# Modulation rows summed on VectorE from tiles turned through DRAM, in place of sum and bias products on TensorE

## The reference, cut to what matters

```python
def modulation(silu_cond, w_mod_l, b_mod_l):
    m = silu_cond @ w_mod_l + b_mod_l            # (1024) @ (1024, 6144) + (6144)
    return jnp.split(m[:, None, :], 6, axis=-1)

def run_layer(x, silu_cond, lw, rope, ctx):
    sh1, sc1, g1, sh2, sc2, g2 = modulation(silu_cond, lw['w_mod'], lw['b_mod'])
    out, ctx_tensors = token_mixer(modulate(x, lw['norm1'], sh1, sc1), lw, rope, ctx)
    x = x + g1 * out
    x = x + g2 * moe_ffn(modulate(x, lw['norm2'], sh2, sc2), lw)
    return x, ctx_tensors
```

## Time and profile before

| What | Value |
|---|---|
| median of three runs | 1472.4 us |
| profiled execution, its own time | 1473.27 us |
| its span | 1471.3 us |
| TensorE busy | 1327.3 us (90%) |
| VectorE, ScalarE, GpSimd busy | 476.2, 328.4, 256.9 us |
| weight loads on SyncE's queue | 327.33 MB, 58.6% of 16 engines' span |
| mean granted clock of TensorE | 0.986 |

### The profile page before, as it was taken

How to read it: one execution, slowest core, us unless ns; L and a number is a source line. 1 busy time by engine, 2 the same in 40 slices (tenths; PEclk the granted TensorE clock), 3 DMA queues, 4 the chain that set the end, 5 groups by cost and what they waited for, 6 DMA issues and landing times.

```text
span 1471.3 us, 17933 instructions
## 1 busy us (share of the span) xinstructions
PE 1327.3 (90%) x7009; PEld 746.0 (51%) x7010; DVE 476.2 (32%) x855; ACT 328.4 (22%) x505; POOL 256.9 (17%) x225
## 2 busy tenths in 40 slices
PE   6999999999999977689899999999999988997772
PEld 2655446675545443345446554555654554553341
DVE  2424326762144101111144352576413521110003
ACT  2136416631001000000021662464100110000001
POOL 2620017721001000000037000683100010000001
PEclk9999999999999999999999999999999999999996
DMA  9781426553829899999973221466412589999994
GB/s 346 257 295 66 172 86 218 212 186 143 281 102 380 336 396 396 396 395 390 361 252 125 94 82 57 173 230 228 158 58 114 224 348 379 405 389 391 399 412 178
DMA packets 105726, 371.90 MB, mean 253 GB/s; under 512 B 7376, under 2 KB 22064, under 8 KB 89280
## 3 DMA queue, kind: packets, MB, share of 16 engines
q1 hardware_dynamic: 84816, 327.33, 58.6%
q0 software_dynamic: 6928, 23.98, 4.5%
q10 hardware_dynamic: 13920, 19.74, 3.9%
HBM read 341.60 MB, written 29.43 MB: 252 GB/s over the span
## 4 chain that ended last, share of the span: by engine, by line
PE 75%; DMA 17%; DVE 4%; ACT 1%; issue 1%; SPq 1%; ACTq 0%; POOL 0%; DVEq 0%; POOLq 0%
PE pG L1587 25%; PE pG L1579 10%; DMA ring<-in_w_exp_down_dram 9%; PE pS L1676 8%; PE pG L1828 6%; PE pG L1692 5%; DMA hT_gen<-in_w_exp_up_dram 3%; DMA ring<-in_w_exp_up_dram 3%; PE pG L1540 3%; PE pX L1507 2%; PE pX L1676 2%; DMA ring<-in_w_mod_dram 2%; PE pX L1656 2%; PE pS L1656 2%; PE pS L1601 2%; PE pX L1642 1%
## 5 line engine op out<-in xcount | busy, mean ns | idle before, releaser
L1587 PE MATMUL pG<-hT_gen,ring 128*128 128x384 f32 x1024 | 339.6, 489 | 1.6 <-ACT hT_gen L955 1.6
L1587 PEld LDWEIGHTS pG<-hT_gen,ring 128*128 128x128 f32 x1024 | 191.8, 190 | 134.5 <-issue 6.6
L1676 PE MATMUL pS<-ring,hT_gen 128*64 128x256 f32 x1408 | 160.1, 383 | 27.6 <-DMA ring<-in_w_exp_up_dram 15.2
L1579 PE MATMUL pG<-ring,hT_gen 128*128 128x512 f32 (+1 forms) x384 | 148.7, 543 | 1.8 <-DVE hT_gen L1112 1.6
L1676 PEld LDWEIGHTS pS<-ring,hT_gen 128*64 128x64 f32 x1408 | 101.8, 138 | 91.9 <-DMA ring<-in_w_exp_up_dram 19.7
L1467 DVE TENSOR_TENSOR hT_gen<-pS,hT_gen 128x256 f32<-128x256 f32 x32 | 19.3, 602 | 371.2 <-PE pS L1676 371.2
L1579 PEld LDWEIGHTS pG<-ring,hT_gen 128*128 128x128 f32 x384 | 71.5, 190 | 70.0 <-issue 64.3
L741 POOL DMA_INDIRECT hT_gen<-y_scr,idx x12 | 11.4, 950 | 515.3 <-ACTq L1020 512.2
L1692 PE MATMUL pG<-ring,hT_gen 128*64 128x512 f32 x352 | 82.1, 608 | 18.6 <-issue 8.2
L982 ACT COPY hT_gen<-pG 128x512 f32<-128x512 f32 x32 | 18.8, 586 | 300.2 <-PE pG L1692 300.2
L1828 PE MATMUL pG<-ring 128*128 128x512 f32 x192 | 83.3, 593 | 2.5 <-DVE ring L1351 2.5
(11 more groups left out here) (282 smaller groups left out, 1643.9 us busy)
## 6 DMA issues: line engine op xcount, KB each, us to landing
ring<-in_w_mod_dram SPq DMA_DIRECT2D x24, 2048.0 KB, 8.2
ring<-in_w_exp_up_dram SPq DMA_DIRECT2D x22, 2048.0 KB, 33.6
ring<-in_w_exp_down_dram SPq DMA_DIRECT2D x22, 2048.0 KB, 34.9
ring<-in_w_exp_gate_dram SPq DMA_DIRECT2D x22, 2048.0 KB, 27.6
ring<-in_w_in_dram SPq DMA_DIRECT2D x20, 2048.0 KB, 7.9
modb<-in_w_exp_gate_dram SPq DMA_DIRECT2D x10, 2048.0 KB, 34.2
hT_gen<-in_w_exp_up_dram SPq DMA_DIRECT2D x10, 2048.0 KB
rows_nw<-in_w_exp_down_dram SPq DMA_DIRECT2D x10, 2048.0 KB, 38.2
```

The lines of the kernel that those rows point to most:

```text
L1579: ins = pe.matmul(ps[:, 0:width], hT[:, k, t * P:(t + 1) * P], w[:, k, 0:width], start=(k == 0), stop=(k == KC - 1))
L1587: ins = pe.matmul(ps[:, 0:TOK], w[:, k, c0:c0 + P], src[:, k, :], start=(k == 0), stop=(k == nk - 1))
L1676: ins = pe.matmul(dst[64 * hf:64 * hf + 64, 0:256], x[:, k, :], w[:, k, 256 * hf:256 * (hf + 1)], start=(k == 0), stop=(k == KC - 1))
```

## The change

The row tiles lose their sum product, and their bias products. The four partial sums of a row tile stay in `modb` as before; ScalarE stores eight rows of it (four parts, two conditions) to a scratch tensor in DRAM (`parts_store`), loads them back turned, so that 64 partitions hold 8 columns each of one condition and 64 those of the other (`parts_load`, two DMAs of 256 pieces of 32 bytes), VectorE adds the four parts and the bias (`mod_rows`), and ScalarE stores the two rows to `mod_scr` (`row_store`, two DMAs of 64 pieces). In the loop over levels the three stages of a tile stand 1, 2 and 5 steps behind its products, VectorE's sum 4. The bias of the row tiles is loaded at the start in four further DMAs of GpSimd. Column tiles are as before.

```diff
...
 def mod_groups(first, last):
-    return [(kind, m + i) for m in range(first, last, 2) for kind in ("mod", "ms") for i in range(2)]
+    return [("mod", m) for m in range(first, last)]
 def groups(L):
     def after(m):
-        return ("mc" if m in COL_MODS else "ms", m)
-    gs = [g for m in range(MOD_FIRST) for g in (("mod", m), after(m))] if L == 0 else []
+        return [("mc", m)] if m in COL_MODS else []
+    gs = [g for m in range(MOD_FIRST) for g in [("mod", m)] + after(m)] if L == 0 else []
...
-        gs += [("ga", j)] + [after(m - 1)] * (j > 0) + [("mod", m)]
-    return (gs + [after(m)] + [("wba", j) for j in range(KC)] + [(k, j) for j in range(KC) for k in ("gh", "wbh")]
+        gs += [("ga", j)] + (after(m - 1) if j > 0 else []) + [("mod", m)]
+    return (gs + after(m) + [("wba", j) for j in range(KC)] + [(k, j) for j in range(KC) for k in ("gh", "wbh")]
...
 O_BANK = (6, 7, 2)
-SMALL_LOADS = 16 * 9
+SMALL_LOADS = 16 * 13
...
+    part_scr = nc.dram_tensor("part_scr", [2, 4, 2, 512], F32, kind="Internal").ap()
+        mparts = sb("mparts", [P, 2, 4, 8])
+        mrow = sb("mrow", [P, 2, 8])
+        mbias = sb("mbias", [P, DEPTH, 8, 8])
...
                             pool.dma_start(dst[:, l, :], a[name][l:l + 1, :].broadcast_to([P, w])).then_inc(small_in, 16)
                     pool.dma_start(wr[:, :, :], a["w_router"].rearrange("(p k) e -> p k e", p=P)).then_inc(small_in, 16)
                     pool.dma_start(br[:, :], a["b_router"].rearrange("(a e) -> a e", a=1).broadcast_to([P, NE])).then_inc(small_in, 16)
+                    for l in range(DEPTH):
+                        for cnd in range(2):
+                            pool.dma_start(mbias[64 * cnd:64 * (cnd + 1), l, :, :],
+                                           a["b_mod"][l, 512 * MOD_FIRST:512 * MODS].rearrange("(u j i) -> j u i", j=64, i=8)
+                                           ).then_inc(small_in, 16)
                     pool.dma_start(masks[:, :, :].rearrange("p s t -> p (s t)"), a["masks"]).then_inc(small_in, 16)
                 pool.wait_ge(h_ready, 2 * NT * L + NT)
...
                 elif m >= 2:
-                    act.wait_ge(mod_stored[m % 2], mods_stored(m, m % 2))
+                    act.wait_ge(part_out[m % 2], 16 * rows_before(m, m % 2))
                 act.copy(mod_parts(m), ps).then_inc(mod_evac, 1)
-            def mod_store(L, m):
-                ps = sync_group(L, ("ms", m))
-                r = 32 * (m % 2)
-                act.copy(mod_parts(m)[r:r + 32, :], ps[r:r + 32, :]).then_inc(ms_evac, 1)
-                act.wait_ge(ms_evac, ROW_MODS.index(m) + 1)
+            def parts_store(m):
+                b = m % 2
+                act.wait_ge(mod_evac, m + 1)
+                act.wait_ge(part_in[b], 32 * rows_before(m, b))
+                act.dma_start(part_scr[b].rearrange("q c n -> (q c) n"),
+                              modb[0:P:16, 2, 0, 512 * b:512 * (b + 1)]).then_inc(part_out[b], 16)
+            def parts_load(m):
+                b = m % 2
+                act.wait_ge(part_out[b], 16 * (rows_before(m, b) + 1))
+                act.wait_ge(mod_summed, max(ROW_MODS.index(m) - 1, 0))
                 for cnd in range(2):
-                    dst = mod_scr[m // MODS, cnd:cnd + 1, 512 * (m % MODS):512 * (m % MODS + 1)]
-                    act.dma_start(dst, mod_parts(m)[r + 16 * cnd:r + 16 * cnd + 1, :]).then_inc(mod_stored[m % 2], 16)
+                    act.dma_start(mparts[64 * cnd:64 * (cnd + 1), b, :, :],
+                                  part_scr[b, :, cnd, :].rearrange("q (j i) -> j q i", i=8)).then_inc(part_in[b], 16)
+            def row_store(m):
+                b = m % 2
+                act.wait_ge(mod_summed, ROW_MODS.index(m) + 1)
+                for cnd in range(2):
+                    dst = mod_scr[m // MODS, cnd, 512 * (m % MODS):512 * (m % MODS + 1)]
+                    act.dma_start(dst.rearrange("(j i) -> j i", i=8),
+                                  mrow[64 * cnd:64 * (cnd + 1), b, :]).then_inc(mod_stored[b], 16)
+            def rows_step(L, i):
+                for delay, stage in ((1, parts_store), (2, parts_load), (5, row_store)):
+                    m = MOD_LEV * (L + 1) + i - delay
+                    if 0 <= i - delay < KC and m in ROW_MODS:
+                        stage(m)
+            def rows_behind(L, kind, stage):
+                if L == 0:
+                    for m in range(MOD_BEHIND[kind], MOD_BEHIND[kind] + 2):
+                        stage(m)
             def mods_behind(L, kind):
...
                     m = MOD_BEHIND[kind]
                     mod_copy(L, m)
                     mod_copy(L, m + 1)
-                    mod_store(L, m)
-                    mod_store(L, m + 1)
+                    parts_store(m)
+                    parts_store(m + 1)
             def hT_half(n, t):
                 act.wait_ge(hT_made, 2 * NT * n + 2 * t + 2)
...
                         att(L, ATT_AT[(kind, h)])
+                        if h == 1:
+                            rows_behind(L, "hq", (parts_load, row_store)[d])
                     mods_behind(L, kind)
                     act.wait_ge(f_done, 2 * HH * L + HH * (d + 1))
                     if d == 0:
...
                     ps = sync_group(L, ("i", t))
                     act.copy(v_rows[:, t, :], ps).then_inc(vrow_ready, 1)
...
+                    if t == 1:
+                        rows_behind(L, "fb", parts_load)
                 mods_behind(L, "i")
                 for t in range(NT):
...
                     act.activation(sg[:, t, :], ps, ACT.Sigmoid).then_inc(sig_done, 1)
                     if ("g", t) in ATT_AT:
...
+                rows_behind(L, "fb", row_store)
                 for j in range(KC):
                     ps = sync_group(L, ("ga", j))
                     act.activation(mergedT[:, j, :], ps[:, 0:TOK], ACT.Sigmoid).then_inc(ga_ready, 1)
                     m = MOD_LEV * (L + 1) + j
-                    if j > 0 and m - 1 in ROW_MODS:
-                        mod_store(L, m - 1)
+                    rows_step(L, j)
                     lev(L, j + 1)
                     mod_copy(L, m)
-                if m in ROW_MODS:
-                    mod_store(L, m)
+                rows_step(L, KC)
                 act.wait_ge(lv_mm, LEV_TILES * L + NT * (LEV_STEPS - 1))
                 act.activation(E[1].rearrange("p (s t) -> p s t", s=SEG), Cs[1][:, :, 0:128], ACT.Exp)
                 for d in range(2):
                     ins = act.activation(dec[:, d, :], Cs[d][:, :, 128], ACT.Exp)
                 ins.then_inc(fin_E, 1)
+                rows_step(L, KC + 1)
                 act.wait_ge(fin_D, 2 * L + 1)
                 act.activation(E[0], E[0], ACT.Exp).then_inc(fin_E, 1)
+                rows_step(L, KC + 2)
                 act.wait_ge(lv_mm, LEV_TILES * (L + 1))
                 act.activation(W[1].rearrange("p (s t) -> p s t", s=SEG), Cs[0][:, :, 1:129], ACT.Exp).then_inc(fin_E, 1)
                 act.wait_ge(fin_D, 2 * L + 2)
                 act.activation(W[0], W[0], ACT.Exp).then_inc(fin_E, 1)
+                rows_step(L, KC + 3)
+                rows_step(L, KC + 4)
                 act.wait_ge(st_ready, 4 * L + 2)
                 for d in range(2):
                     dst = (new_sf, new_sb)[d][0, L].rearrange("h k v -> k h v")
...
                     ins = dve.scalar_tensor_tensor(dst, ps, 1.0, bc(nwT[:, l, k0:k0 + 4], [P, 4, 2], 2),
                                                    ALU.add, ALU.mult)
                 ins.then_inc(mc_evac, 1)
+            def mod_rows(m):
+                b, l = m % 2, m // MODS
+                dve.wait_ge(part_in[b], 32 * (rows_before(m, b) + 1))
+                dve.wait_ge(mod_stored[b], mods_stored(m, b))
+                link(dve.tensor_reduce(mrow[:, b, :], mparts[:, b, :, :].rearrange("p q i -> p i q"), AX.X, ALU.add))
+                dve.tensor_tensor(mrow[:, b, :], mrow[:, b, :], mbias[:, l, m % MODS - MOD_FIRST, :],
+                                  ALU.add).then_inc(mod_summed, 1)
+            def mod_rows_of(L, j):
+                m = MOD_LEV * (L + 1) + j
+                if m in ROW_MODS:
+                    mod_rows(m)
             def norm1_mean(L, t):
                 dve.wait_ge(sq_done, NT * 2 * L + t + 1)
...
                         dve.tensor_scalar(x, x, omT[:, L, d, h:h + 1], lbT[:, L, d, h:h + 1], ALU.mult,
                                           ALU.add).then_inc(f_done, 1)
                         att(L, ATT_AT[(kind, h)])
+                    if L == 0 and d == 0:
+                        for m in range(MOD_BEHIND["hq"], MOD_BEHIND["hq"] + 2):
+                            mod_rows(m)
                     dve.wait_ge(ln_done, 2 * L + d + 1)
                     for s in range(SEG):
                         dve.tensor_tensor_scan(Cs[d][:, s, 1:129], ones, scratch[:, s * P:(s + 1) * P], 0.0,
...
```

(28 more changed lines are left out.)

9 lines of the change are left out of this document (6 added, 3 removed).

## The result

| | before | after |
|---|---|---|
| median of 7 runs each, in turns on one chip, us | 1473.14 (1471.92 to 1475.96) | 1479.09 (1476.53 to 1480.83) |
| ratio, 95% interval | | 1.0033 (1.002 to 1.0046) |
| profiled execution: span, us | 1471.3 | 1476.7 |
| VectorE instructions / packets on ScalarE's DMA queue | 855 / 13920 | 887 / 25376 |

A forecast was written before the change was run, and what follows sets the result against it. TensorE was taken to bound projections and loops, DMA the experts. Gains of 4.5, 3.8 and 4.1 us (12.4) less 3.6 lost made 8.8 us faster: 1463.5 us, range 1457.5 to 1471.5.

The forecast's parts named there:

- the pairs in layer 0: Row tiles 4 to 7, two pairs in layer 0's projections, where TensorE is full: 4.5 us gained without sums and bias products.
- the start: Four bias loads on GpSimd ahead of the masks; delay up to some 8 us hidden by gaps: 0.4 us lost.
- rival (b): Small bias pieces at the start are dear, each microsecond beyond 8 us of delay is lost; chance 0.08.
- the cost behind layer 0's loop: Two issues on ScalarE behind layer 0's loop over levels: 0.5 us lost.
- the upper end of my sum (16): Whole kernel: the favourable ends of all terms together give 16 us gained, the other ends 1 us.
- the clock: Longer TensorE idle behind both loops lowers the granted clock: between 0 and 3 us lost, taken as 1.0.
- the wait at the end: Behind layer 1's loop: 0.7 us lost to issues, 1.0 to the last tile's load waiting for its own store.
- the price of an issue: ScalarE in the loops: 0.3 us for the part store, 0.45 for two loads, 0.4 for two row stores, each issue.
- the path: Loop: gate group's end through ScalarE's issues and exponentials to VectorE's products, 10.6 us, or 11.4 with row stores.
- The circle: Loop from step 4: loads wait for VectorE's earlier sum, exponentials queue behind them; 11.6 us a step, 10.8 in step 4.
- what I called wrong (12): Sign against the forecast: loop steps above 12 us with VectorE waiting for a DMA.
- rival (a): Transfers land late in the loop, sums wait for row stores; harmless below 9 us, at 12.4 us 1500 us; chance 0.09.

The follow-up runs named there:

- batching: Changed kernel with only part stores in the loop; one load, reduction, addition and row store per layer for all eight tiles: 1458.83 us (0.9891), again 1461.23 (0.9905).
- the kernel with issues put back: Batched kernel plus four DMA issues of 64 pieces behind each part store in the loop, which nobody waits for: 1475.63 us, ratio 1.0009 to the kernel before.
- both deep: Changed kernel with a place of its own for every summed row and every tile of turned parts: 1473.13 us, ratio 0.9986 to the kernel before.
- one issue each: Both deep, with one DMA instead of two for the load of parts and one for the row store: 1471.72 us, ratio 0.9985.
- the addition behind the masks: Both deep, with VectorE's sum and bias of a tile behind the masks and one step later: 1473.47 us, ratio 0.999.
- the end put off: Both deep, with last loads behind the last store, row stores behind ScalarE's squares, sums of tiles 4 to 7 among VectorE's gate products: 1467.90 us, ratio 0.9948.
- batched, 4 more issues of one row: Batched kernel plus four DMA issues of one unbroken 2 KB row behind each part store in the loop: 1466.67 us, ratio 0.995.

## Why the prediction was wrong

Right were: the pairs in layer 0 (4.50 us, forecast 4.5); the start (0.57, forecast 0.4), so the delay of rival (b) did not show here; the cost behind layer 0's loop (0.58, forecast 0.5); the order of events in a late step; and the upper end of my sum (16), which batching nearly reached.

Against the forecast the account of the first section is 14.3 us worse: 6.3 in the two loops, 6.0 at the end of layer 1, 1.7 in the two stretches that I had left to the clock, and 0.3 elsewhere. So two steps of the prediction failed, the pace of a step in the loops and the wait at the end.

**The first: the price of an issue.** I put store, load and row store between one row (0.245) and 512 pieces (0.466), at 0.3, 0.45 and 0.4. They measured 0.59, 0.64 and 0.62. Per step that is 3.1 us instead of 2.0. With it, the path is 11.5 - 2.15 + 3.1 = 12.5 instead of 11.4. It is a size that was off, in the term on which the sum of the loops rested most. That issue time is what moves these loops is shown by the kernel with issues put back. How much of the 6.3 us is this 1.1 us a step is not shown: against both deep, one issue each made the loops of layers 1 and 0 shorter by 1.7 us and by nothing, the addition behind the masks by 2.3 and 1.6, batching by 5.2 and 3.1. I had taken the nearest rows for bounds, and they were none: an issue's time did not follow the number of pieces. One of 64 pieces of 32 bytes (0.62) was dearer than one of 512 pieces in the row of before, and one load of all parts (0.45) cheaper than each of its halves (0.64).

**The circle** exists, but it does not set the step. With 0.8 more for its four issues and 1.0 more for the addition, my 11.6 becomes 13.4 us a step. From one start of the level products to the next, layer 1 has 10.4, 10.6, 10.8, 10.7, 11.7, 13.0 and 10.1 us in the trace; I had reckoned 10.15, 10.15, 10.4, 10.4, 10.8, 11.6 and 11.6. So one late step was above what I called wrong (12), but with VectorE waiting for ScalarE and not for a DMA. With the waits for places taken out (both deep) the same late steps are 11.7, 13.0 and 10.1 again. With the addition behind the masks they are 10.5, 12.0 and 10.0, and batched 10.0, 10.4 and 10.0. What the circle costs beyond the issues and the addition that stand in it is therefore nothing that these traces can tell.

**The small instruction.** "Two small instructions of 0.17 us" was read from a row where GpSimd was idle. In the loop the addition ended with GpSimd's running subtraction and took 1.2 to 1.3 us in some steps, ahead of the masks that TensorE's level products wait for. The Trainium skill states in "SBUF — State Buffer", section on the two separate sides, that VectorE operations with two SBUF inputs and GpSimd operations that read SBUF lock each other out for a whole instruction. By that rule, the trace agrees: the addition (two inputs) ended with GpSimd's operation, the reduction (one input) took 0.20 us beside the same one.

**The second: the landing at the end of layer 1.** I allowed 1.0 us, for the load of the last tile behind its own part store. Another transfer decided: the sum of tile 20 waits for the row store of tile 18. In the circle I had that wait, "issued one step earlier", and rival (a) made it harmless below 9 us. That holds as long as a full step lies between. In the last two steps VectorE has no products any more, it comes to the sum at once, and 7.9 us of landing are bare: from 1008.16 to 1016.10, about the 7.7 us that the earlier trace rows had shown for stores. ScalarE's last part store stood until 1015.73 behind the load of tile 21, a wait for a place in the scratch that I had not counted at all. Where rival (a) would have cost every step, landing cost one place, 7.66 us instead of 1.7; that it is the landing is shown by the end put off, where the stretch is 11.81 us. Outside such a stretch the landings were short: 2.2 and 2.3 us in the median. The Trainium skill's figure of about 2 us for the fixed cost of a transfer, in "DMA: Bandwidth & Descriptors", section on the anatomy of one DMA, is given there for DMAs that GpSimd issues. On ScalarE's queue these medians agree with it, and the 7.6 and 8.7 that the same two lines show at worst do not; the DMA share from 1002 to 1020 us is 0.98.

**The clock** I put at 1.0 us in all, behind the loops. There it cost nothing new, as shown above. What was lost lies later, ahead of the experts of each layer, where 24 products take 4.33 us instead of 2.94 in layer 0 and 4.34 instead of 2.94 in layer 1; from 465 to 467 us the granted clock was 0.50, where it was 1.00 before.

```profile
465.19 4.33 PE pG L1750 x24
...
1185.38 4.34 PE pG L1750 x24
```

In layer 0 they took 4.58 batched, with 0.71 us idle behind the loop, and 2.94 with both deep, with 1.28, so it does not follow from that wait. What it follows from stays open.

**The range** rested on 0.25 to 0.55 us an issue. With the measured price and the longer addition my own sum gives 0.4 us gained in layer 0's loop (0.15 lost was measured) and 1.5 lost in layer 1's (1.8 gained), 1472.5 in all; with the measured landing, 6 us more, 1478.5. That this is near the measured 1479.09 is in part luck, since it is 3.3 us too dear in layer 1's loop and leaves out 1.7 us of clock. Issues and addition together take most of the forecast gain of the loops away, and the landing makes the loss. The chance of 0.10 for slower was far too low for a path whose main term no row of before showed.

Open: how much of the 7 us between the changed kernel and both deep is the waits for places and how much the group of runs (their traces differ by 1.8 us at the end and 0.6 in the loops); how the 6.3 us of the loops divide between issues and addition; and what sets an issue's time. I have only the forms above.

## What to carry to other kernels

Count the DMA issues that a change puts on a computing engine as busy time of that engine, price them by a row of the very same form, and if there is none, take a multiple of the nearest one as the upper end. If an engine's path has no room in the loop, leave in the loop only what frees a buffer and do the rest once, behind it, as batched. And where a wait for a landing is hidden by other work, look at the last steps apart: there that work is gone, and the landing is bare.

## What the runs showed of the hardware

- The time of an issue on ScalarE's queue, median: one unbroken row of 2 KB 276 ns; 64 pieces of 32 bytes 617 ns; both halves in one issue of 128 pieces 428 ns; eight tiles in one load of 128 KB 372 ns; a store from 8 partitions of 2 KB 552 to 586 ns. The loads of 256 pieces took 638 ns, of 512 in one issue 454. Above one row, more bytes or more pieces did not make an issue dearer; in the median the forms over all 128 partitions took 0.37 to 0.47 us and those over 8 or 64 took 0.55 to 0.64, which is a pattern of these rows and not shown to be the cause.
- A VectorE addition of 128x8 took 1.20 and 1.32 us in two late steps beside GpSimd's subtraction, 1.95 in one place of the kernel with the sum behind the masks, and ended each time within 0.02 us of GpSimd's operation; its median is 0.17.
- Small transfers on ScalarE's queue of the changed kernel landed after 2.2 and 2.3 us in the median and after 7.6 and 8.7 us at worst, beside weight loads on SyncE's queue (DMA share 0.98).
- Short waits of TensorE inside a dense loop cost more than their length: with 6.9 us of waits for VectorE in layer 1's loop (batched, 4 more issues of 64 pieces) the granted clock was 0.85 and 0.83 over two stretches of 10 us, with 1.6 us of waits (batched) 1.00 in the same ones; the loop was 8.8 us longer for 5.3 us more of waits. With 6.0 us (batched, 4 more issues of one row) it was 0.83 over one such stretch. The changed kernel, with 5.8, stayed at 1.00, so it is not their sum alone.
